# Gate projections by seven quarter products, with the modulation sums on other stages, in a two-layer hybrid trunk step

## What is computed

```python
mod = silu(cond) @ ada_w + ada_b                 # 6 * 1024 columns, for each of the two conditionings
sh_a, sc_a, gt_a, sh_m, sc_m, gt_m = split(mod, 6)
h = x * (1 + sc_a) + sh_a
aq, ak, av, ag, lr_f, lr_b, bz, cq, ck, cv, mg = split_cols(h @ w_in, IN_WIDTHS)   # mg: 3 * 1024 columns
br_a = gated linear attention(aq, ak, av, ag, lr_f, lr_b)       # 512 channels
br_b = chunked gMLP(bz)                                          # 512 channels
br_c = windowed attention(cq, ck, cv)                            # 512 channels
gates = sigmoid(mg).reshape(tokens, 3, 1024)
proj = einsum('lnc,ncd->lnd', [br_a, br_b, br_c], w_branch)
y = sum(gates * proj, axis=branch) @ w_out
x = layer_norm(alpha * x + gt_a * y)
... then sc_m, sh_m, router, 16 experts (top 2), gt_m, layer_norm
```

## Time and profile before

| | |
|---|---|
| time of a launch, median of 3 runs | 2103.98 us (2101.12 to 2105.12) |
| profiled execution, span | 2100.0 us |
| TensorE (PE) busy | 2010.4 us, 96% |
| VectorE (DVE) busy | 964.4 us, 46% |
| ScalarE (ACT) busy | 486.3 us, 23% |
| merge stage of layer 0 | 313 to 715 us of the span |
| merge stage of layer 1 | 1355 to 1752 us |

### The profile page before, as it was taken

How to read it: one execution, slowest core, us unless ns; L and a number is a source line. 1 busy time by engine, 2 the same in 40 slices (tenths; PEclk the granted TensorE clock), 3 DMA queues, 4 the chain that set the end, 5 groups by cost and what they waited for, 6 DMA issues and landing times.

```text
span 2100.0 us, 25029 instructions
## 1 busy us (share of the span) xinstructions
PE 2010.4 (96%) x9957; PEld 1348.4 (64%) x9957; DVE 964.4 (46%) x2068; ACT 486.3 (23%) x778; POOL 140.3 (7%) x198
## 2 busy tenths in 40 slices
PE   6999999999999998999889999999999999999995
PEld 3787776677767786333457877766677677853333
DVE  1136118667766776111172350286677316651116
ACT  1241103433420001111143411134334200101112
POOL 2000000000010003000030000000000000020001
PEclk8999999999999999999999999999999999989998
DMA  9691112324243515998671111124232422369994
GB/s 371 217 333 48 33 51 72 126 90 141 74 163 128 211 54 206 357 365 331 250 267 60 61 50 32 50 73 143 82 133 72 170 81 100 119 229 355 368 341 171
DMA packets 169509, 345.31 MB, mean 164 GB/s; under 512 B 10865, under 2 KB 124081, under 8 KB 159729
## 3 DMA queue, kind: packets, MB, share of 16 engines
q1 hardware_dynamic: 141712, 248.97, 33.5%
q0 software_dynamic: 21024, 72.00, 9.3%
q10 hardware_dynamic: 6656, 22.71, 2.7%
HBM read 286.17 MB, written 60.10 MB: 165 GB/s over the span
## 4 chain that ended last, share of the span: by engine, by line
PE 83%; DMA 8%; DVE 6%; ACT 1%; issue 1%; POOL 1%; SPq 0%; POOLq 0%; DVEq 0%; ACTq 0%
PE PS L1044 78%; DMA store<-in_expert_w_up_dram 4%; PE PS L1048 4%; DMA ar<-in_ada_w_dram 1%; DVE ar L1725 1%; DMA mg<-rows_h,idxi 1%; DMA xr<-out_y_dram 1%; DVE xr L549 1%; ACT store L1514 0%; POOL rows L1016 0%; DMA mg<-rows,posi 0%; DVE store L1725 0%; ACT ar L1514 0%; DMA store<-rows,posi 0%; PE PS L558 0%
## 5 line engine op out<-in xcount | busy, mean ns | idle before, releaser
L1044 PE MATMUL PS<-store 128*128 128x320 f32 (+2 forms) x4192 | 1102.0, 424 | 2.6 <-DVE ar L1725 1.7
L1044 PEld LDWEIGHTS PS<-store 128*128 128x128 f32 (+1 forms) x4192 | 780.7, 189 | 297.1 <-issue 19.1
L1044 PE MATMUL PS<-store,mg 128*64 (+2 forms) x2152 | 499.1, 536 | 22.1 <-DMA store<-in_expert_w_up_dram 12.3
L1044 PEld LDWEIGHTS PS<-store,mg 128*64 128x64 f32 (+1 forms) x2152 | 233.6, 155 | 236.7 <-issue 211.9
L549 DVE SCALAR_TENSOR_TENSOR xr<-store,cs,xr 128x256 f32<-128x256 f32 x560 | 246.7, 482 | 10.0
L1514 ACT ACTIVATE xr<-PS 128x256 f32<-128x256 f32 (+1 forms) x108 | 56.1, 525 | 554.8 <-PE PS L1044 554.8
L1514 ACT ACTIVATE ar<-PS 128x640 f32<-128x640 f32 (+4 forms) x131 | 86.8, 694 | 373.1 <-PE PS L1048 188.9
L1725 DVE TENSOR_TENSOR mg<-PS,mg 128x256 f32<-128x256 f32 x33 | 14.0, 425 | 317.4 <-ACT mg L1514 317.4
L1514 ACT ACT_TABLE_LOAD x112 | 143.7, 1283 | 2.0
L1725 DVE TENSOR_TENSOR ar<-PS,xr 128x640 f32<-128x640 f32 x32 | 26.4, 825 | 153.2 <-PE PS L1044 153.2
L1514 ACT ACTIVATE mg<-PS 128x256 f32<-128x256 f32 x66 | 25.4, 384 | 241.6 <-PE PS L1044 223.3
(11 more groups left out here) (249 smaller groups left out, 1408.1 us busy)
## 6 DMA issues: line engine op xcount, KB each, us to landing
store<-in_w_in_dram SPq DMA_DIRECT2D x50, 1024.0 KB, 7.3
store<-in_ada_w_dram SPq DMA_DIRECT2D x43, 1024.0 KB, 5.0
store<-in_expert_w_gate_dram SPq DMA_DIRECT2D x33, 1024.0 KB, 8.5
store<-in_expert_w_up_dram SPq DMA_DIRECT2D x33, 1024.0 KB, 10.8
store<-in_expert_w_down_dram SPq DMA_DIRECT2D x33, 1024.0 KB, 5.6
rows<-const POOLq DMA_DIRECT2D x2, 8960.0 KB, 36.4
rows<-ar ACTq DMA_DIRECT2D x33, 512.0 KB, 8.9
mg<-rows SPq DMA_DIRECT2D x27, 512.0 KB, 11.9
```

The lines of the kernel that those rows point to most:

```text
L1044: return nc.tensor.matmul(out, lhsT, rhs, start=start, stop=stop, skip_group_check=True)
```

## The change

Gate blocks are made two at a time (`gates`, 256 columns, weights W and inputs H each cut in 2 x 2 quarters of 512 channels by 128 columns or 320 tokens) by the Winograd form of Strassen's product: 7 products of 4 matmuls, in place of 8. The sums of quarters of H are made once per layer on VectorE (four of 128x1280: `turn1`, `turn2`, `ht4`, `h12`), two of them copied by ScalarE in units 3 and 4; the sums of quarters of W are four VectorE operations of 128x512 for each pair of steps (`weights_summed_first`, `weights_summed_last`, in the ring slot itself). Parts that two outputs share are copied out of PSUM by ScalarE (`gate_parts`, four of 320 columns) and added on VectorE (`gate_parts_added`, four of 320 columns); Sigmoid then runs on `sig` in place (`gates_opened`).

The order of the merge is new: pairs of gates stand in units 0, 2, 4, 6, 8, 10, 13, 16 and 19, the branches of a pair in the units behind it. The steps go through branches and halves of the 1024 columns in another order, four at a time. The rotations stand in units 0 and 2 (three each), the norms in units 0 and 2. Modulation blocks 8 to 23 stand in steps 4 to 19 in both layers. The first 8 for layer 1 are made in layer 0 during the first projections (`mods_early`): 16 instructions of VectorE each. The ring has 5 slots; the sixth holds `first_acc`, and then `ht4` and `ws1`.

```diff
-RING = 6
+RING = 5
+HOME_PARTS = 6
...
 def rot_beside(u):
-    return (2 * u, 2 * u + 1) if u < 3 else ()
+    return {0: (0, 1, 2), 2: (3, 4, 5)}.get(u, ())
 def merge_step(m):
-    n, r = divmod(m, 8)
-    return r // 4, (1, 0, 2)[n], r % 4
+    run, q = divmod(m, 4)
+    half, n = ((0, 1), (0, 0), (1, 1), (1, 0), (0, 2), (1, 2))[run]
+    return half, n, q
+def gates_beside(u):
+    if u < 12:
+        return u if u % 2 == 0 else None
+    return {13: 12, 16: 14, 19: 16}.get(u)
+def branches_beside(u):
+    if u < 11:
+        return (u - 1, u) if u % 2 else ()
+    return {11: (10,), 12: (11,), 14: (12,), 15: (13,), 17: (14,), 18: (15,)}.get(u, ())
 def heads_beside(u):
-    return {2: (0, 1), 5: (2, 3)}.get(u, ())
+    return {0: (0, 1), 2: (2, 3)}.get(u, ())
+MOD_FROM = 4
+def mod_beside(m):
+    return MOD_FIRST + m - MOD_FROM if MOD_FROM <= m < MOD_FROM + MOD_ALL - MOD_FIRST else None
+def mods_early(l, after):
+    if l == DEPTH - 1:
+        return ()
+    return {("ak", 0): (0,), ("ak", 1): (1,), ("tok", 0): (2,), ("tok", 1): (3,), ("tok", 2): (4,), ("tok", 3): (5,), ("u", 1): (6, 7)}.get(after, ())
...
# TensorE
+                def gates(m):
                     half, n, q = merge_step(m)
                     w = view(on.wait_block(pe, ("mg", half, n, q // 2)), KD)
-                    feature_major(("gate", half, n, q), w, h3, slice(P * (q % 2), P * (q % 2) + P))
+                    pair = m // 2
+                    turn1, turn2 = ht12[m // 8 > 0]
+                    x = on.wait_slot(pe, ("gate", half, n, q))
+                    left, right = x[:, 0:HALF], x[:, 512:512 + HALF]
+                    product(left, w[:, 0:4, 0:P], h11, True, True).then_inc(on.product, 1)
+                    product(right, w[:, 4:8, 0:P], h21, True, True).then_inc(on.product, 1)
+                    y = on.wait_slot(pe, ("gate", half, n, q + 1))
+                    low, high = y[:, 0:HALF], y[:, 512:512 + HALF]
+                    pe.wait_ge(on.summed, weights_summed(m, 0))
+                    product(low, ws1, turn1, True, True).then_inc(on.product, 1)
+                    product(high, w[:, 4:8, P:2 * P], ht4, True, True)
+                    pe.wait_ge(on.summed, weights_summed(m, 1))
+                    pe.wait_ge(on.kept, kept_count(m, 1))
+                    product(left, w[:, 0:4, 0:P], turn2, False, True).then_inc(on.product, 1)
+                    pe.wait_ge(on.kept, kept_count(m, 2))
+                    product(low, w[:, 4:8, 0:P], h22, False, True)
+                    pe.wait_ge(on.kept, kept_count(m, 3))
+                    product(left, w[:, 0:4, P:2 * P], h12, False, True).then_inc(on.filled, 2)
...
# VectorE, unit u, behind the softmax of the unit
-                    if gate_beside(u) is not None:
-                        conditioned(gate_beside(u))
                     for head in heads_beside(u):
                         head_gated(head)
                     for c in rot_beside(u):
                         rotated(c)
-                    if branch_beside(u) is not None:
-                        gated(branch_beside(u))
+                    if gates_beside(u) is not None:
+                        weights_summed_last(gates_beside(u))
                     if u:
                         values_moved(u - 1)
+                    if gates_beside(u) is not None:
+                        pair_gated(gates_beside(u))
+                    if next_pair(branches_beside(u)) is not None:
+                        weights_summed_first(next_pair(branches_beside(u)))
+                    for m in branches_beside(u):
+                        gated(m)
...
+                def weights_summed_last(m):
...
+                    dve.wait_ge(on.product, 4 * (m // 2) + 1)
+                    step(tt(w[:, 0:4, 0:P], ws1, w[:, 0:4, 0:P], ALU.subtract))
+                    dve.wait_ge(on.product, 4 * (m // 2) + 2)
+                    tt(w[:, 4:8, 0:P], w[:, 4:8, 0:P], w[:, 0:4, 0:P], ALU.subtract).then_inc(on.summed, 1)
+                def gate_parts_added(m, part):
...
+                    if part == 0:
...
+                        tt(sig[0][:, 0:HALF], x[:, 512:512 + HALF], sig[0][:, 0:HALF], ALU.add)
+                        return
+                    on.wait_filled(dve, ("gate", half, n, q + 1))
+                    dve.wait_ge(on.kept, kept_count(m, 3))
+                    tt(sig[0][:, HALF:TOK], y[:, 0:HALF], sig[0][:, HALF:TOK], ALU.add).then_inc(on.gate_ready, 1)
+                    dve.wait_ge(on.gate_ready, 5 * pair + 2)
+                    tt(sig[1][:, HALF:TOK], x[:, 0:HALF], sig[1][:, HALF:TOK], ALU.add)
+                    tt(sig[1][:, 0:HALF], y[:, 512:512 + HALF], sig[1][:, 0:HALF], ALU.add).then_inc(on.dve_moved, 2)
...
+                def pair_gated(m):
+                    ada, ada1 = mod_beside(m), mod_beside(m + 1)
+                    if ada is not None:
+                        conditioned(ada, acc)
+                    gate_parts_added(m, 0)
+                    if ada1 is not None:
+                        step(row_sums(step, on.wait_block(dve, ("ada", ada1)), acc[ada1 % 2], range(0, KD // 2)))
+                    gate_parts_added(m, 1)
+                    if ada1 is not None:
+                        row_sums(step, on.ring_slot(("ada", ada1)), acc[ada1 % 2], range(KD // 2, KD)).then_inc(on.acc_ready, 1)
```

311 lines of the change are left out of this document (210 added, 101 removed).

## The result

The changed kernel took 2142.64 us (median of 4 runs, 2140.86 to 2142.81), the kernel before 2104.55 in the runs beside them (4 runs, 2101.12 to 2107.89): a ratio of 1.0181 [1.0164, 1.0198]. That is 38 us slower. I had forecast "slower" as the likeliest sign, but 2118 as the time, and 2132 as the end of the range.

A forecast was written before the change was run, and what follows sets the result against it. TensorE was taken to bound the merge, with VectorE nearly full. Span 2100.0 - 52.5 (matmuls) + 60.6 (merge waits) + 5.3 (early modulation) + 0.8 (end of layer 0) = 2114.2 us, median 4.0 above: 2118; range 2078 to 2132.

The forecast's parts named there:

- What bounds the kernel: In the merge TensorE (PE) sets the pace; VectorE has 30% left, nearly no room after the change.
- Waits of the merges, 60.6 us: Both merges: PE waits 32.1 us per merge against 1.8 before, 30.3 more each, 60.6 in two layers.
- waits of units 0 to 3: Start of each merge: lost cover for ScalarE's norms and VectorE's rotations makes PE wait 15.6 us.
- wait per pair: Merge, behind each gate pair: PE waits 1 to 1.5 us for VectorE's 320-column additions to free PSUM slots.
- it cancels: Rival: merge waits 10 us fewer leave 2104 plus or minus 4 us; chance 0.17.
- the clock falls, or loads show: Rival: four PE gaps in units 0 and 2 at 2 us each, and late ada blocks, 2130 to 2145; chance 0.08.
- 52.5 us saved by the form: Gate pairs, both layers: 28 matmuls in place of 32, 2.19 us less per pair, 52.5 us in all.
- I count the loads as hidden, and 0 to 8 us for the range: Early layer 0: 8 MB of ada blocks sharing the queue with the zero fill cost nothing, 0 to 8 us in the range.
- Waits for `ada` blocks: Sign in the new profile that the prediction is wrong: waits for the loads of modulation blocks.
- Early modulation, 5.3 us: Early layer 0: block 7's row sums delay the statistics and block 6's move; PE waits some 5.3 us.
- The rivals that ended faster: VectorE keeps up: 2085 us median, or 2070 if units 0 and 2 also hide half; chance of below 2099.8: 0.31.
- the likeliest case: Whole kernel: the time comes out as worked out, 2108 to 2130 us; chance 0.44.

The follow-up runs named there:

- rot_last: The changed kernel with the three rotations of units 0 and 2 each put behind the gate pair; 2136.57 us, ratio 1.0162.
- warm_half: The changed kernel with 13 unread matmuls (6, 4 and 3) in each merge, in the gaps of units 0 and 2; 2142.02 us, ratio 1.0192.
- one_row_sums: The changed kernel with VectorE's row sums beside the gate pairs cut to the first of 8 rows per modulation block; 2174.76 us, ratio 1.0326.
- sums_later: short_chain with 2 instead of 4 of the 8 rows of a pair's second modulation block ahead of the last additions; 2103.32 us, ratio 0.999.
- spread_all: The changed kernel with the zero_late and stats_first edits, and the rotations spread over units 0 to 3 ahead of the mean squares; 2107.01 us, ratio 1.001.
- eight_spread: spread_all with gate pairs made of eight quarter products again and no sums of blocks; 2122.1 us, ratio 1.009.
- zero_late: The changed kernel with GpSimd's copy of x and zero fill issued after the state stores; 2135.71 us, ratio 1.0139.
- stats_first: The changed kernel with block 7's row sums and the moves of modulation blocks 6 and 7 behind the statistics; 2137.51 us, ratio 1.0155.
- short_chain: spread_all with two additions behind a pair's last product, in place of a copy and three additions; 2099.93 us, ratio 0.9981.

## Why the prediction was wrong

*What bounds the kernel.* Right: PE, with VectorE as the engine that makes it wait.

*Waits of the merges, 60.6 us.* Right, 59.9 measured, though the sum is closer than its parts. In the merge of layer 0 the waits of units 0 to 3 are 13.6 us (15.6 forecast), and the rest of its 33.5 us of idle time is 19.9 (16.5 forecast for the pairs behind them, and the kernel before has 3.7 in the whole stretch). The wait per pair is there at 1.5 to 1.7 us (forecast 1.2 to 1.9), the one for the values behind pair 16 at 2.8 (2.6), the one of 3.8 us for ScalarE's Exp at the third rotation of unit 0 (3.9), 2.4 and 1.9 in unit 2 (2.9 and 2.9); the 1.6 for weight sums ahead of product 5 in unit 0 did not come here, but did once PE was there sooner (1.53 in rot_last, 1.11 in warm_half). An addition of 320 columns took 0.486 us (0.49 to 0.5 taken). VectorE was busy 160.5 of 200 us between 450 and 650, 80%, where I had said above 85%; the load matters all the same (one_row_sums, sums_later), because its work comes at fixed places. "Waits 10 us fewer" in the rival "it cancels" is a slip of the sum, which gives 2108; 2104 takes the 14 that the prediction names itself.

*"Four such gaps at 2 us each", in the rival "the clock falls, or loads show", chance 0.08.* This is the step that failed in the merges: I priced gaps by their own length in the sum and kept the clock out of it, though the earlier trace rows showed 0.93 where the kernel before has gaps. Of the 14.2 us by which the saving of matmuls fell short, 6.8 are this: spreading the rotations brought 3.4 us of busy time a merge back (spread_all), and filling the gaps restored the durations of the rows. The Trainium skill ("TensorE: Matmul & The Clock Gate", part 1, section "What's actually happening") has the clock drop after idleness and come back after sustained work; I had weighed it and left it out of the sum, and these rows agree with it.

*52.5 us saved by the form.* Mis-sized for another reason too, which makes nearly all of the rest: with the clock level, 96 rows fewer took 22.9 us out of a merge (eight_spread against spread_all), and not 26.3, so 6.7 us in two layers. Why stays open. Eight rows show as 2.42 us behind some waits where 2.32 is usual, but they do so behind the scores of unit 2 too, without a wait.

*"I count the loads as hidden, and 0 to 8 us for the range."* This is the step that failed in the early part, and the larger one: 10.2 us, shown by zero_late (with the 2 to 3 us by which this stretch differs between profiles). I knew the DMA share of 0.75 in that stretch, and took it as room; it was the mean of a full and an empty part. It was the fill itself, and the new blocks met it. Waits for `ada` blocks were named as a sign of being wrong, and this sign came.

*Early modulation, 5.3 us.* The place was right. It cost 7.7 us (stats_first): 3.3 of idle time, and 4.4 of busy time, which the sum had at nothing and which is certain only to 1.2. It and the loads overlap by 5 us (spread_all), so the two don't add up to the 13.5 missed.

*The rivals that ended faster* (0.31) needed VectorE to keep up; one_row_sums shows that even an eighth of the row sums leaves half of the waits for quarter sums. *Chance of 0.08 for 2130 to 2145*: the case happened with both of its halves, the clock and the late loads, and lay at its upper end; the likeliest case was given 0.44.

The change can be made to pay, though hardly: with the four mended places (short_chain) it took 2099.93 us, 0.9981 [0.997, 0.9992] of the kernel before, and as sums_later 0.999 [0.9978, 1.0002], which is level.

## What to carry to other kernels

Room on average does not hide a new load that starts inside a large transfer: look at what the DMA engines move at the time when it is issued, and put a fill that nobody waits for where they are idle. When work is packed to make place for a longer block, price the gaps twice, once by their length and once by the rows behind them. An arithmetic trick that takes 1/8 of the matmuls and puts additions on an in-order engine that is already 70% busy kept 15 and 21 us of its 52 here, in two orders of the work around it: count that engine's work per unit before the matmuls. And what is moved to make place for it has a price of its own, here 59 us as first written and 18 when mended.

## What the runs showed of the hardware

Two 1 MB loads beside fills of 8960 KB from another queue took 26.2 and 19.5 us to land, against a median of 5.0, with the DMA share at 1.04 between 100 and 160 us; with the fills moved away such loads took at most 10.3. After PE gaps of 3.8 us, or of 2.4 and 1.9 close together, the next 16 rows of 320 columns took 5.41 and 6.17 us in place of 4.47; behind gaps of 1.5 us 32 rows took the usual 8.88. Unread matmuls in the gap were enough to keep the rows at 4.5 us.
